# Gathering the tokens of two experts in one pass of 256-column matmuls

## The chip, the cores and the metric

The kernel runs on one core of a Trainium2 chip. The metric is the device time of one execution in microseconds (us). The kernel before takes 1973.86 us, the median of three runs (1971.27 to 1975.2). A "hi" and a "lo" below are the two fp32r parts of an fp32 number: every product of two fp32 matrices is computed as three fp32r matmuls (lo by hi, hi by lo, hi by hi).

## The reference, cut to what matters

Two decoder layers over 16 + 256 tokens of 1024 features. The first ends in a dense SwiGLU, the second in a mixture of 8 experts, of which each token takes its best two. The change touches the mixture alone:

```
probs = softmax(t @ w_router)                    # 256 tokens, 8 experts
top_p, top_i = top_k(probs, 2); top_p /= sum(top_p)
combine = sum(one_hot(top_i, 8) * top_p[..., None], axis=1)
for e in range(8):
    out += combine[:, e] * ((silu(t @ w_gate[e]) * (t @ w_up[e])) @ w_down[e])
```

with w_gate and w_up of 1024 x 3584 and w_down of 3584 x 1024 for each expert, all in fp32.

## The kernel before, in words

From about 923 us on the kernel works through the experts in turn. For each expert g it gathers the chosen tokens, at most 128 of them, into 128 slots, computes the expert for these slots, and scatters the weighted result back to the 256 tokens. (An expert with more than 128 tokens gets a further group at the end, under an If; the traced run has eight gathers, so none was taken.)

**Gather** (TensorE `gather`, L906 to L915). The selection matrix S (tokens by slots, ones and zeros; VectorE `places`, L1894, makes it with two compares) is the moving operand, 128 columns; the tokens x_hi and x_lo (2 tiles of 128 tokens each) are the stationary one. Four sources by eight blocks of 128 features are 32 matmuls at L914, which fill two banks of PSUM, X = ps[1][2:4]. ScalarE copies these to xg_hi in one instruction of 1024 columns (L1309, reached through `copy`, L1017), and VectorE subtracts to get xg_lo (L1905). For the first expert the matmuls wait for x_hi and x_lo one by one.

**An expert** is cut into seven chunks of 512 hidden columns. On TensorE a chunk (L942 to L957) is: gate, 24 matmuls of 512 columns into bank ps[0][0]; `turn`, four transposes of the hidden values of the chunk before into bank TB = ps[0][2] (L887); up, 24 matmuls into ps[0][1]; then `down` for the chunk before, 24 matmuls (L899, L901, L902) into Y = ps[1][0:2]. Chunk 0 of an expert closes the down product of the expert before it (the seam). Chunk 1 scatters the result of the expert before, into ps[0][2:4] and X. Chunk 6 begins with `slots` (L922, L924): the weight of each slot and the transpose of S go into bank MISC = ps[0][3], and ScalarE copies them out as slot_w and ST. The gather of the next expert stands in chunk 6 between up and down (L954).

**Weights** come in units of 1 MB: 6 units a chunk, 42 an expert. SyncE loads a unit into one of six raw buffers; ScalarE copies it to w_hi (L1017, from `hi_at`), VectorE subtracts to w_lo (L1566), each in one of three buffers; TensorE uses it in 12 matmuls and releases it (`units_used`). So the work of ScalarE and VectorE on a unit starts when TensorE has released the unit three places ahead of it. The instructions of each engine run in the order written; what ScalarE and VectorE do besides (ag_hi, g_sl, xg_hi on ScalarE; ag_lo, a_sl, xg_lo on VectorE) stands at fixed places between the units. In the first chunk of an expert, xg_hi comes between the first and second unit of ScalarE (L1271) and xg_lo between those of VectorE (L1851).

**Loops.** Experts 1 to 6 are one loop on each engine, with an inner loop over chunks 2 to 5; experts 0 and 7 are written out before and after it. What the loops wait on is worked out in registers from the loop's variables.

Of the kernel before, what the change touches and what calls it, by code (L numbers as in the profile page):

```python
# [50 lines left out]
START = 1  # L51

# [43 lines left out]
def trunk(nc, w, consts, where, out):  # L96

    ctx = ExitStack()
    with ctx:
# [100 lines left out]
        S = sb(moe, "S", [P, 2, P], F32R)  # L200
        ST = sb(moe, "ST", [P, 2, P], F32R)
        xg_hi = sb(moe, "xg_hi", [P, KT, P], F32R)
        xg_lo = sb(moe, "xg_lo", [P, KT, P], F32R)
# [274 lines left out]
        def norm_tmp(norm, a, b):  # L478

            if norm == 1:  # L480
                return (gT_s, aT_f)[a // 4][:, a % 4:a % 4 + b - a, width(0)]
            return sgA[:, a:b, width(norm // 2)]

# [105 lines left out]
        def _(pe):  # L589
# [283 lines left out]
            def gate_or_up(dst, at, u):  # L873
                for i in range(2):
                    u_hi, u_lo = expert_unit(at + i, u + i)
                    for k in range(4):
                        last = mm3(dst, xg_hi[:, 4 * i + k, :], xg_lo[:, 4 * i + k, :],
                                   u_hi[:, k * COLS:(k + 1) * COLS], u_lo[:, k * COLS:(k + 1) * COLS],
                                   start=(i == 0 and k == 0), stop=(i == 1 and k == 3))
                    last.then_inc(units_used, 1)  # L880
# [37 lines left out]
            def slots(g, e):  # L918

                pe.wait_ge(scatter_added, START + 2 * g + 2)  # L920
                for t in range(2):
                    nc.tensor.matmul(MISC[:, 0:1], S[:, t, :].bitcast(F32), comb[:, t, bass.ds(e, 1)], start=(t == 0), stop=(t == 1))  # L922
                for t in range(2):
                    last = nc.tensor.transpose(MISC[:, (t + 1) * P:(t + 2) * P], S[:, t, :].bitcast(F32), ident)  # L924
                last.then_inc(slots_full, 1)
# [12 lines left out]
            def expert(g, e, seam=False, more=False):  # L938

                u0, k0, at = NS + g * UPG, g * JCH, NS  # L940

                def chunk(j, first=False, final=False, scatters=False, last=False):  # L942
                    uj, k = u0 + (j * UPJ - 2), k0 + j
                    if last:
                        slots(g, e)
# [3 lines left out]
                    gate_or_up(U_, at + 6, uj + 2)  # L949
# [9 lines left out]
                pe.wait_ge(gather_hi_ready, START + g + 1)  # L959
                pe.wait_ge(gather_lo_ready, START + g + 1)  # L960
                if seam:
                    chunk(0, final=True)
                else:
                    pe.wait_ge(silu_ready, START + k0)
                    gate_or_up(G_, at, u0)
                    pe.wait_ge(hidden_ready, START + k0)
                    gate_or_up(U_, at + 2, u0 + 2)
                chunk(1, first=True, scatters=seam)
# [14 lines left out]
            gather(0, True)  # L983
# [3 lines left out]
            expert(0, 0, more=True)  # L987
            with pe.Fori(1, EXPERTS - 1) as g:
                expert(g, g, seam=True, more=True)
            expert(EXPERTS - 1, EXPERTS - 1, seam=True)  # L990
# [4 lines left out]
            for s in range(SPILLS):  # L995
                with pe.If(n_groups > s):
                    gather(EXPERTS + s, spilled=True)
                    expert(EXPERTS + s, spill[s])
# [6 lines left out]
        def _(act):  # L1005
# [253 lines left out]
            def expert(g, e, seam=False):  # L1259
# [7 lines left out]
                def chunk(j, gathers=False, scatters=False, last=False):  # L1267
                    uj, k, turns = u0 + (j * UPJ - 2), k0 + j, j - 1
                    hi_of(g, 4, turns, uj)
                    if gathers:  # L1270
                        gathered(g)  # L1271
                    hi_of(g, 5, turns, uj + 1)
                    if scatters:
                        result(g, uj)
                    if last:
                        act.wait_ge(slots_full, START + g + 1)
                        act.wait_ge(result_lo_ready, START + g + 1)
                        copy(slot_w[:, :], ps[0][:, 3, 0:1])
                        copy(ST[:, :, :], ps[0][:, 3, P:3 * P].rearrange("p (t s) -> p t s", t=2)).then_inc(slots_ready, 1)
                    for i in range(2, 4):  # L1280
                        hi_of(g, 4 + i, turns, uj + i)
                    turned(k - 1, uj)
                    silu(k, uj + 2)
                    for i in range(4, 6):
                        hi_of(g, 4 + i, turns, uj + i)

                if seam:
                    chunk(0, gathers=True)
# [17 lines left out]
            def gathered(n):  # L1306

                act.wait_ge(gather_full, START + n + 1)
                copy(xg_hi[:, :, :], ps[1][:, 2:4, :].rearrange("p b (k s) -> p (b k) s", s=P)).then_inc(gather_hi_ready, 1)  # L1309
# [13 lines left out]
            expert(0, 0)  # L1323
            with act.Fori(1, EXPERTS) as g:
                expert(g, g, seam=True)
# [3 lines left out]
            for s in range(SPILLS):  # L1329
                with act.If(n_groups > s):  # L1330
                    expert(EXPERTS + s, spill[s])
# [7 lines left out]
        def _(dve):  # L1339
# [498 lines left out]
            def expert(g, e, seam=False, more=False):  # L1838
# [8 lines left out]
                def chunk(j, start=0, gathers=False, scatters=False, last=False):  # L1847
                    uj, k = u0 + (j * UPJ - 2), k0 + j
                    for i in range(start, 4):
                        if i == 1 and gathers:  # L1850
                            gathered(g)  # L1851
                        if i == 2 and scatters:
                            result(g)
                        if i == 2 and last and more:
                            places(g + 1, g + 1, e + 1, 0)
# [10 lines left out]
                if seam:  # L1866
                    chunk(0, gathers=True)
                    chunk(1, scatters=True)
                else:
                    if type(g) is int and g == 0:  # L1870
                        gathered(0)
                        lo(3, u0 + 3)
                    else:
                        places(g, g, e, P)
                        gathered(g)
                        for i in range(4):
                            lo(i, u0 + i)
# [16 lines left out]
            def places(n, slots_read, e, first_slot):  # L1894

                dve.wait_ge(gather_full, START + n)
# [5 lines left out]
            def gathered(n):  # L1902

                dve.wait_ge(gather_hi_ready, START + n + 1)
                tt(xg_lo[:, :, :], ps[1][:, 2:4, :].rearrange("p b (k s) -> p (b k) s", s=P), xg_hi[:, :, :].bitcast(F32),  # L1905
                   ALU.subtract).then_inc(gather_lo_ready, 1)
# [19 lines left out]
            places(0, 0, 0, 0)  # L1926
# [23 lines left out]
            expert(0, 0, more=True)  # L1950
            with dve.Fori(1, EXPERTS - 1) as g:
                expert(g, g, seam=True, more=True)
            expert(EXPERTS - 1, EXPERTS - 1, seam=True)
            last_down(EXPERTS - 1)
            n_groups, spill = load_plan(dve)
            for s in range(SPILLS):
                with dve.If(n_groups > s):
                    expert(EXPERTS + s, spill[s])
# [30 lines left out]
```

## Time and profile before

| | us |
|---|---|
| median of three runs | 1973.86 |
| the profiled execution, whole | 1971.98 |
| its span, first to last instruction | 1970.0 |
| TensorE busy in the span | 1888.0 (96%) |
| VectorE busy | 1382.9 (70%) |
| ScalarE busy | 1114.6 (57%) |

The chain of work that ended last gives 52% of the span to TensorE and 1% to VectorE. A matmul's duration in the trace holds its way through the array, and the next one starts long before it ends; what a matmul costs in a sequence is the distance from its start to the next one's start. Rows with a count (x16) merge neighbours of one kind. Each row has start, duration, engine, line, operation, out<-in and count; what stands in brackets is idle time and what ended it.

### The profile page before, as it was taken

How to read it: one execution, taken by the hardware profiler on the slowest of the kernel's cores; microseconds unless marked ns; L12 is line 12 of the kernel's file. 1: busy time of each engine (PE TensorE's matmuls, PEld its weight loads, DVE VectorE, ACT ScalarE, POOL GpSimd, SP SyncE). 2: the span in 40 equal slices, each digit the busy share in tenths (PEclk: the TensorE clock that was granted, in tenths of full speed). 3: DMA queues.
4: the chain of work that ended last, by engine and by line, in shares of the span. 5: the costliest groups of instructions: out<-in, count | busy, mean ns of one | idle time of the engine just before them, and what ended most of it. 6: DMA issues, size and time to landing. Idle time of an engine off the chain costs nothing.

```text
span 1970.0 us, 28868 instructions
## 1 busy us (share of the span) xinstructions
PE 1888.0 (96%) x11195; PEld 1664.4 (84%) x11195; DVE 1382.9 (70%) x1134; ACT 1114.6 (57%) x850; POOL 6.3 (0%) x15
## 2 busy tenths in 40 slices
PE   7999999899989899998999999999999999999995
PEld 6889999899988899997888888888888888888883
DVE  2555556644554556566788888888888888888885
ACT  3634344533454453444777667776767677676773
POOL 0000000000000000000000000000000000000000
PEclk9889999999998999997999999999999999999998
DMA  9636633454566548343899999999999999999991
GB/s 218 182 107 184 160 124 134 150 171 147 183 110 155 145 124 204 125 169 124 297 365 333 354 359 327 367 340 347 357 332 360 334 351 361 337 348 349 337 366 73
DMA packets 218448, 488.19 MB, mean 248 GB/s; under 512 B 7884, under 2 KB 12744, under 8 KB 218360
## 3 DMA queue, kind: packets, MB, share of 16 engines
q1 hardware_dynamic: 216464, 482.44, 73.3%
q10 hardware_dynamic: 1400, 2.33, 0.5%
q0 software_dynamic: 496, 2.17, 0.3%
q8 instruction: 66, 1.08, 0.2%
q14 instruction: 22, 0.18, 0.0%
HBM read 483.66 MB, written 1.05 MB: 246 GB/s over the span
## 4 chain that ended last, share of the span: by engine, by line
PE 52%; DVE 1%; issue 0%; ACT 0%; DVEq 0%; ACTq 0%
PE ps L595 11%; PE ps L597 11%; PE ps L596 11%; PE ps L899 5%; PE ps L902 5%; PE ps L901 5%; PE ps L914 1%; PE ps L887 1%; PE ps L934 0%; PE ps L839 0%; PE ps L935 0%; DVE w_lo L1566 0%; PE ps L848 0%; PE ps L922 0%; DVE h_tok L1545 0%
## 5 line engine op out<-in xcount | busy, mean ns | idle before, releaser
L1566 DVE TENSOR_TENSOR w_lo<-raw,w_hi 128x2048 fp32r<-128x2048 f32 x336 | 763.3, 2289 | 153.9 <-ACT w_hi L1017 152.4
L1017 ACT ACTIVATE w_hi<-raw 128x2048 fp32r<-128x2048 f32 x336 | 639.1, 1918 | 197.9 <-PE ps L902 103.8
L595 PE MATMUL ps<-hT_hi,w_lo 128*128 128x272 f32 (+1 forms) x1392 | 407.7, 293 | 27.4 <-DVE hT_lo L1518 13.6
L361 DVE TENSOR_TENSOR w_lo<-raw,w_hi 128x2048 fp32r<-128x2048 f32 (+2 forms) x131 | 279.4, 2143 | 217.1 <-ACT w_hi L354 211.7
L596 PE MATMUL ps<-hT_lo,w_hi 128*128 128x272 f32 (+1 forms) x1392 | 406.0, 292 | 0.0
L597 PE MATMUL ps<-hT_hi,w_hi 128*128 128x272 f32 (+1 forms) x1392 | 405.4, 291 | 0.0
L595 PE MATMUL ps<-w_hi,xg_lo 128*128 128x512 f32 x896 | 361.0, 403 | 3.2 <-DVE xg_lo L1905 3.2
L597 PE MATMUL ps<-w_hi,xg_hi 128*128 128x512 f32 x896 | 355.1, 396 | 0.0
L596 PE MATMUL ps<-w_lo,xg_hi 128*128 128x512 f32 x896 | 354.9, 396 | 0.0
L354 ACT ACTIVATE w_hi<-raw 128x2048 fp32r<-128x2048 f32 (+2 forms) x131 | 233.9, 1793 | 183.0 <-PE ps L597 140.7
L595 PEld LDWEIGHTS ps<-hT_hi,w_lo 128*128 128x128 f32 x1392 | 269.2, 193 | 32.3 <-issue 22.6
L596 PEld LDWEIGHTS ps<-hT_lo,w_hi 128*128 128x128 f32 x1392 | 268.9, 193 | 0.1
L597 PEld LDWEIGHTS ps<-hT_hi,w_hi 128*128 128x128 f32 x1392 | 268.2, 193 | 0.0
L595 PEld LDWEIGHTS ps<-w_hi,xg_lo 128*128 128x128 f32 x896 | 169.2, 189 | 41.0 <-issue 3.6
L597 PEld LDWEIGHTS ps<-w_hi,xg_hi 128*128 128x128 f32 x896 | 169.1, 189 | 40.8
L596 PEld LDWEIGHTS ps<-w_lo,xg_hi 128*128 128x128 f32 x896 | 169.4, 189 | 37.4
L899 PE MATMUL ps<-w_hi,ag_lo 128*128 128x512 f32 x448 | 177.6, 396 | 1.8 <-DVE ag_lo L1835 1.8
L901 PE MATMUL ps<-w_lo,ag_hi 128*128 128x512 f32 x448 | 177.1, 395 | 0.0
L902 PE MATMUL ps<-w_hi,ag_hi 128*128 128x512 f32 x448 | 177.1, 395 | 0.0
L899 PEld LDWEIGHTS ps<-w_hi,ag_lo 128*128 128x128 f32 x448 | 84.2, 188 | 25.9 <-DVE ag_lo L1835 2.0
L902 PEld LDWEIGHTS ps<-w_hi,ag_hi 128*128 128x128 f32 x448 | 84.2, 188 | 20.1
L901 PEld LDWEIGHTS ps<-w_lo,ag_hi 128*128 128x128 f32 x448 | 84.3, 188 | 18.0
(260 smaller groups left out, 1867.3 us busy)
## 6 DMA issues: line engine op xcount, KB each, us to landing
raw<-in_moe_w_gate SPq DMA_DIRECT2D x112, 1024.0 KB, 7.1
raw<-in_moe_w_up SPq DMA_DIRECT2D x112, 1024.0 KB, 7.3
raw<-in_moe_w_down SPq DMA_DIRECT2D x112, 1024.0 KB, 6.2
raw<-in_w_in SPq DMA_DIRECT2D x63, 1024.0 KB, 8.6
raw<-in_ffn_w_gate SPq DMA_DIRECT2D x10, 1024.0 KB, 5.1
raw<-in_ffn_w_up SPq DMA_DIRECT2D x10, 1024.0 KB, 5.1
raw<-in_ffn_w_down SPq DMA_DIRECT2D x10, 1024.0 KB, 5.1
raw<-in_w_pa SPq DMA_DIRECT2D x8, 1024.0 KB, 5.1
```

Of the source, the lines that this page charges most:

```text
L354: nc.scalar.activation(w_hi[:, u % HALVES, 0:k * n], raw[:, u % RAW, 0:k * n], ACT.Copy).then_inc(hi_ready, 1)
L361: nc.vector.tensor_tensor(w_lo[:, u % HALVES, 0:k * n], raw[:, u % RAW, 0:k * n], w_hi[:, u % HALVES, 0:k * n].bitcast(F32), ALU.subtract) ...
L595: nc.tensor.matmul(dst, l_lo, r_hi, start=start, stop=False)
L596: nc.tensor.matmul(dst, l_hi, r_lo, start=False, stop=False)
L597: return nc.tensor.matmul(dst, l_hi, r_hi, start=False, stop=stop)
L887: last = nc.tensor.transpose(TB[:, i * P:(i + 1) * P], a_sl[:, i * P:(i + 1) * P], ident)
L899: last = nc.tensor.matmul(Y[:, q, :], ag_lo[:, 2 * i + kk, :], u_hi[:, o:o + COLS], start=first and i == 0 and kk == 0, stop=False)
L901: nc.tensor.matmul(Y[:, q, :], ag_hi[:, 2 * i + kk, :], u_lo[:, o:o + COLS], start=False, stop=False)
L902: last = nc.tensor.matmul(Y[:, q, :], ag_hi[:, 2 * i + kk, :], u_hi[:, o:o + COLS], start=False, stop=final and i == 1 and kk == 1)
L914: last = nc.tensor.matmul(X[:, k // 4, (k % 4) * P:(k % 4 + 1) * P], x_[:, t, k * P:(k + 1) * P], S[:, t, :], start=(i == 0 and k % 4 == 0 ...
L1017: return nc.scalar.activation(dst, src, ACT.Copy, **kw)
L1566: tt(w_lo[:, at % HALVES, :], raw[:, at % RAW, :], w_hi[:, at % HALVES, :].bitcast(F32), ALU.subtract).then_inc(lo_ready, 1)
```

## The change

The gather is done for two experts at once. S gets a further axis (one selection per expert, 256 columns in all), so do xg_hi and xg_lo. A pair's gather is done in two halves of 16 matmuls with 256 moving columns, one for each half of the features: the first fills ps[1][2:4], as before, the second ps[0][2:4], which are the banks TB and MISC. Each copy out takes one half of the features of one expert (512 columns, in four pieces of 128), so there are four copies on ScalarE and four subtractions on VectorE for a pair where there were two of 1024 columns each. In the first chunk of a pair the first expert's copies stand between the first and second unit, the second expert's between the second and third. ScalarE's copy for the second expert waits until VectorE has read the same banks for the first. The matmuls and copies of the experts are otherwise as before, and so are the weights' loads.

Added waits on TensorE: before a pair's gather, that the hidden values were copied out of TB and the slots out of MISC; before the first `turn` after it, that all four subtractions are done. The loop runs over pairs (1 and 2), its body has two experts; pairs 0 and 3 are written out.

```diff
-        S = sb(moe, "S", [P, 2, P], F32R)
+        S = sb(moe, "S", [P, 2, 2, P], F32R)
...
-            def gather(n, first_gather=False, spilled=False):
+            def gather(m, n, first_gather=False, spilled=False):
-                pe.wait_ge(places_ready, START + n + 1)
+                pe.wait_ge(places_ready, START + m + 1)
                 pe.wait_ge(scatter_added, START + 2 * n + (2 if spilled else 0))
-                for i, (x_, t) in enumerate(((x_hi, 0), (x_hi, 1), (x_lo, 0), (x_lo, 1))):
-                    if first_gather:
-                        pe.wait_ge((x_hi_ready, x_lo_ready)[i // 2], t + 1)
-                    for k in range(KT):
-                        last = nc.tensor.matmul(X[:, k // 4, (k % 4) * P:(k % 4 + 1) * P], x_[:, t, k * P:(k + 1) * P], S[:, t, :],
-                                                start=(i == 0 and k % 4 == 0), stop=(i == 3 and k % 4 == 3))
-                last.then_inc(gather_full, 1)
+                for half in range(2):
+                    for i, (x_, t) in enumerate(((x_hi, 0), (x_hi, 1), (x_lo, 0), (x_lo, 1))):
+                        if first_gather and half == 0:
+                            pe.wait_ge((x_hi_ready, x_lo_ready)[i // 2], t + 1)
+                        for k in range(4):
+                            f = (4 * half + k) * P
+                            last = nc.tensor.matmul(ps[1 - half][:, 2 + k // 2, (k % 2) * 2 * P:(k % 2 + 1) * 2 * P], x_[:, t, f:f + P],
+                                                    S[:, t, :, :].rearrange("p e s -> p (e s)"),
+                                                    start=(i == 0 and k % 2 == 0), stop=(i == 3 and k % 2 == 1))
+                    last.then_inc(gather_full, 1)
...
                     pe.wait_ge(silu_ready, START + k)
-                    gate_or_up(G_, at + 4, uj)
+                    gate_or_up(G_, at + 4, uj, o)
+                    if moved:
+                        pe.wait_ge(gather_lo_ready, START + 4 * m + 4)
                     turn(k - 1)
...
                     if last and more:
-                        gather(g + 1)
+                        pe.wait_ge(hidden_lo_ready, START + k)
+                        pe.wait_ge(slots_ready, START + g + 1)
+                        gather(m + 1, g + 1)
...
-            with pe.Fori(1, EXPERTS - 1) as g:
-                expert(g, g, seam=True, more=True)
+            with pe.Fori(1, PAIRS - 1) as m:
+                expert(m, m * 2, m * 2, 0, seam=True)
+                expert(m, m * 2 + 1, m * 2 + 1, 1, seam=True, more=True)
...
@@ ScalarE, an expert's chunk
                     hi_of(g, 4, turns, uj)
                     if gathers:
-                        gathered(g)
+                        gathered(m, 0)
                     hi_of(g, 5, turns, uj + 1)
+                    if gathers:
+                        gathered(m, 1)
...
@@ ScalarE, expert 0 (not at a seam)
-                    gathered(g)
-                    for i in range(HALVES if type(g) is int and g == 0 else 0, 4):
+                    gathered(m, 0)
+                    for i in range(HALVES if m == 0 else 0, 4):
                         hi_of(g, i, 0, u0 + i)
+                    gathered(m, 1)
                     silu(k0, u0 + 2)
...
+            def gathered(m, o):
+                for half in range(2):
+                    act.wait_ge(gather_full, START + 2 * m + half + 1)
+                    if o:
+                        act.wait_ge(gather_lo_ready, START + 4 * m + half + 1)
+                    copy(xg_hi[:, o, 4 * half:4 * half + 4, :], gathered_in(half, o)).then_inc(gather_hi_ready, 1)
...
@@ VectorE: places makes both experts' selections
-                for t in range(2):
-                    ins = ts_(S[:, t, :], iota[:, first_slot:first_slot + P], rank[:, t, bass.ds(e, 1)], None, ALU.is_equal)
+                for t in range(2):
+                    for o, e in enumerate(experts):
+                        ins = ts_(S[:, t, o, :], iota[:, first_slot:first_slot + P], rank[:, t, bass.ds(e, 1)], None, ALU.is_equal)
...
+                    tt(xg_lo[these], gathered_in(half, o), xg_hi[these].bitcast(F32), ALU.subtract).then_inc(gather_lo_ready, 1)
```

## Rows read from the trace of the kernel before

**Rows 1.** Busy time by engine in a stretch of expert work: count, clock, DMA share, GB/s.
```profile
core 0: us, PE busy (x) PEld busy (x) DVE busy (x) ACT busy (x) POOL busy (x), PEclk, DMA share, GB/s
1160.00:1800.00 640.00, 640.00 (x2921) 520.43 (x2920) 546.69 (x315) 449.72 (x305) 0.00 (x0) 1.00 0.96 348
```

**Rows 2.** Waits of TensorE, 950 to 1970 us: total, times, longest.
```profile
PE ps L934 <- DVE y_lo L1911: 2.5, 1, 2.5
PE ps L899 <- DVE ag_lo L1835: 1.8, 1, 1.8
```

**Rows 3.** Timeline of TensorE around the gather for expert 2.
```profile
1171.18 0.40 PE L597 MATMUL ps<-w_hi,xg_hi 128*128 128x512 f32 x1
1171.41 1.90 PE L914 MATMUL ps<-S,x_hi 128*128 128x128 f32 x16
1173.15 1.95 PE L914 MATMUL ps<-S,x_lo 128*128 128x128 f32 x16
1174.93 0.45 PE L899 MATMUL ps<-w_hi,ag_lo 128*128 128x512 f32 x1
```

**Rows 4.** Timeline of TensorE: fp32r matmuls of 256 columns, the first and the last of 37.
```profile
897.73 0.28 PE L597 MATMUL ps<-zT_hi,w_hi 128*128 128x256 f32 x1
...
901.99 0.28 PE L597 MATMUL ps<-zT_hi,w_hi 128*128 128x256 f32 x1
```

**Rows 5.** Timeline of TensorE: matmuls of 256 columns whose operands are plain fp32.
```profile
690.45 1.03 PE L743 MATMUL ps<-v_tok,eT 128*128 128x256 f32 x4
691.32 1.03 PE L747 MATMUL ps<-srT,qT 128*128 128x256 f32 x4
```

**Rows 6.** Busy time and clock in the stretch of the first gather; columns as in rows 1.
```profile
926.00:933.00 7.00, 4.26 (x20) 4.08 (x20) 6.18 (x20) 1.65 (x3) 0.00 (x0) 0.50 0.00 0
```

**Rows 7.** Timeline from the first gather to expert 0.
```profile
922.51 0.48 DVE L1899 TENSOR_SCALAR S<-tab,rank 128x128 fp32r<-128x128 f32 x2 [0.79 <-DVE plan_f L1813]
...
923.21 3.64 PE L914 MATMUL ps<-S,x_hi 128*128 128x128 f32 x16
...
926.65 3.62 PE L914 MATMUL ps<-S,x_lo 128*128 128x128 f32 x16
...
929.70 2.29 DVE L1566 TENSOR_TENSOR w_lo<-raw,w_hi 128x2048 fp32r<-128x2048 f32 x1
...
931.91 1.22 DVE L1905 TENSOR_TENSOR xg_lo<-ps,xg_hi 128x1024 fp32r<-128x1024 f32 x1
...
933.49 0.77 PE L595 MATMUL ps<-w_hi,xg_lo 128*128 128x512 f32 x1 [3.23 <-DVE xg_lo L1905]
```

**Rows 8.** Timeline of expert 0's first units, to the start of its chunk 1.
```profile
938.08 1.92 ACT L1017 ACTIVATE w_hi<-raw 128x2048 fp32r<-128x2048 f32 x1 [6.76 <-PE ps L597]
...
943.74 4.50 DVE L1566 TENSOR_TENSOR w_lo<-raw,w_hi 128x2048 fp32r<-128x2048 f32 x2 [1.42 <-ACT w_hi L1017]
...
946.22 0.43 PE L595 MATMUL ps<-w_hi,xg_lo 128*128 128x512 f32 x1
```

**Rows 9.** Groups of instructions, 950 to 1960 us: copies of 512 columns (busy, mean ns).
```profile
L1835 DVE TENSOR_TENSOR ag_lo<-ps,ag_hi 128x512 fp32r<-128x512 f32 x56 | 38.3, 684 | 0.0
...
L1017 ACT ACTIVATE ag_hi<-ps 128x512 fp32r<-128x512 f32 x56 | 33.5, 599 | 72.7 <-PE ps L887 72.7
```

**Rows 10.** Timeline after that gather: third unit of chunk 0, and up.
```profile
1182.82 2.29 DVE L1566 TENSOR_TENSOR w_lo<-raw,w_hi 128x2048 fp32r<-128x2048 f32 x1 [0.52 <-ACT w_hi L1017]
...
1186.54 0.48 PE L595 MATMUL ps<-w_hi,xg_lo 128*128 128x512 f32 x1
```

**Rows 11.** Timeline of an ordinary chunk: the first unit of down.
```profile
1151.08 4.49 DVE L1566 TENSOR_TENSOR w_lo<-raw,w_hi 128x2048 fp32r<-128x2048 f32 x2 [1.32 <-ACT w_hi L1017]
...
1153.33 0.40 PE L597 MATMUL ps<-w_hi,xg_hi 128*128 128x512 f32 x1
...
1153.56 0.39 PE L899 MATMUL ps<-w_hi,ag_lo 128*128 128x512 f32 x1
```

**Rows 12.** Register instructions of ScalarE's wait for a unit (L1022).
```profile
L1022 ACTq ALU_OP  x191: 35/35/53, 958.1 to 1926.5; - x191
```

**Rows 13.** The busiest chunk for the DMA queues; columns as in rows 1.
```profile
1243.00:1260.00 17.00, 17.00 (x77) 13.69 (x76) 14.77 (x8) 12.15 (x9) 0.00 (x0) 1.00 1.01 365
```

More of the change, by code:

```diff
@@ L936, in scatter, with expert, chunk @@
                     last.then_inc(scatter_full, 1)
-            def expert(g, e, seam=False, more=False):
+            def expert(m, g, e, o, seam=False, more=False):
                 u0, k0, at = NS + g * UPG, g * JCH, NS
-                def chunk(j, first=False, final=False, scatters=False, last=False):
+                def chunk(j, first=False, final=False, scatters=False, last=False, moved=False):
                     uj, k = u0 + (j * UPJ - 2), k0 + j
                     if last:
-                        slots(g, e)
+                        slots(g, e, o)
                     pe.wait_ge(silu_ready, START + k)
-                    gate_or_up(G_, at + 4, uj)
+                    gate_or_up(G_, at + 4, uj, o)
+                    if moved:
+                        pe.wait_ge(gather_lo_ready, START + 4 * m + 4)
                     turn(k - 1)
-                    gate_or_up(U_, at + 6, uj + 2)
+                    gate_or_up(U_, at + 6, uj + 2, o)
                     if scatters:
@@ L982, in _ @@
             pe.wait_ge(dve_done, NSETS - 1)
-            gather(0, True)
+            gather(0, 0, True)
             pe.wait_ge(act_done, NSETS)
@@ L986, in _ @@
             pe.wait_ge(comb_ready, 1)
-            expert(0, 0, more=True)
-            with pe.Fori(1, EXPERTS - 1) as g:
-                expert(g, g, seam=True, more=True)
-            expert(EXPERTS - 1, EXPERTS - 1, seam=True)
+            expert(0, 0, 0, 0)
+            expert(0, 1, 1, 1, seam=True, more=True)
+            with pe.Fori(1, PAIRS - 1) as m:
+                expert(m, m * 2, m * 2, 0, seam=True)
+                expert(m, m * 2 + 1, m * 2 + 1, 1, seam=True, more=True)
+            expert(PAIRS - 1, EXPERTS - 2, EXPERTS - 2, 0, seam=True)
+            expert(PAIRS - 1, EXPERTS - 1, EXPERTS - 1, 1, seam=True)
             last_down(EXPERTS - 1)
@@ L996, in _ @@
                 with pe.If(n_groups > s):
-                    gather(EXPERTS + s, spilled=True)
-                    expert(EXPERTS + s, spill[s])
+                    gather(PAIRS + s, EXPERTS + s, spilled=True)
+                    expert(PAIRS + s, EXPERTS + s, spill[s], 0)
                     last_down(EXPERTS + s)
@@ L1257, in turned, with expert @@
                 copy(ag_hi[:, :, :], TB4).then_inc(hidden_hi_ready, 1)
-            def expert(g, e, seam=False):
+            def expert(m, g, e, o, seam=False):
                 u0, k0 = NS + g * UPG, g * JCH
@@ L1322, in _ @@
             act.sem_inc(result_hi_ready, START + 1)
-            expert(0, 0)
-            with act.Fori(1, EXPERTS) as g:
-                expert(g, g, seam=True)
+            expert(0, 0, 0, 0)
+            expert(0, 1, 1, 1, seam=True)
+            with act.Fori(1, PAIRS) as m:
+                for o in range(2):
+                    expert(m, m * 2 + o, m * 2 + o, o, seam=True)
             last_down(EXPERTS - 1)
@@ L1836, in turned, with expert @@
                    ALU.subtract).then_inc(hidden_lo_ready, 1)
-            def expert(g, e, seam=False, more=False):
+            def expert(m, g, e, o, seam=False, more=False):
                 u0, k0 = NS + g * UPG, g * JCH
@@ L1849, in chunk @@
                     for i in range(start, 4):
-                        if i == 1 and gathers:
-                            gathered(g)
+                        if i in (1, 2) and gathers:
+                            gathered(m, i - 1)
                         if i == 2 and scatters:
@@ L1866, in expert @@
                 if seam:
-                    chunk(0, gathers=True)
+                    chunk(0, gathers=(o == 0))
                     chunk(1, scatters=True)
                 else:
[L1870 to L1877, printed above, removed]
+                    if m:
+                        places(m, g, (e,), P)
+                    gathered(m, 0)
+                    for i in range(0 if m else 3, 4):
+                        lo(i, u0 + i)
+                    gathered(m, 1)
                     for i in range(4, 6):
@@ L1892, in last_down, with places, gathered @@
                     add(g + 1, t)
-            def places(n, slots_read, e, first_slot):
-                dve.wait_ge(gather_full, START + n)
+            def places(m, slots_read, experts, first_slot):
+                dve.wait_ge(gather_full, START + 2 * m)
                 dve.wait_ge(slots_full, START + slots_read)
                 for t in range(2):
-                    ins = ts_(S[:, t, :], iota[:, first_slot:first_slot + P], rank[:, t, bass.ds(e, 1)], None, ALU.is_equal)
+                    for o, e in enumerate(experts):
+                        ins = ts_(S[:, t, o, :], iota[:, first_slot:first_slot + P], rank[:, t, bass.ds(e, 1)], None, ALU.is_equal)
                 ins.then_inc(places_ready, 1)
[L1902 to L1906, printed above, removed]
+            def gathered(m, o):
+                for half in range(2):
+                    dve.wait_ge(gather_hi_ready, START + 4 * m + 2 * o + half + 1)
+                    these = (slice(None), o, slice(4 * half, 4 * half + 4))
+                    tt(xg_lo[these], gathered_in(half, o), xg_hi[these].bitcast(F32), ALU.subtract).then_inc(gather_lo_ready, 1)
             def result(n):
@@ L1925, in _ @@
             dve.sem_inc(scatter_added, START + 2)
-            places(0, 0, 0, 0)
+            places(0, 0, (0, 1), 0)
             r = number[1, "x_tok"]
@@ L1949, in _ @@
             lo(HALVES - 1, NS + HALVES - 1)
[L1950 to L1953, printed above, removed]
+            expert(0, 0, 0, 0)
+            expert(0, 1, 1, 1, seam=True, more=True)
+            with dve.Fori(1, PAIRS - 1) as m:
+                expert(m, m * 2, m * 2, 0, seam=True)
+                expert(m, m * 2 + 1, m * 2 + 1, 1, seam=True, more=True)
+            expert(PAIRS - 1, EXPERTS - 2, EXPERTS - 2, 0, seam=True)
+            expert(PAIRS - 1, EXPERTS - 1, EXPERTS - 1, 1, seam=True)
             last_down(EXPERTS - 1)
```

40 lines of the change are left out of this document (20 added, 20 removed).

## The prediction

> **What bounds the kernel now.** I read the windows first, since a change in the expert part can pay only if the engine it relieves never rests there. From 1160 to 1800 us TensorE is busy 640 of 640 us at the full clock; VectorE is at 85% (546.69 / 640), ScalarE at 70% [rows 1]. Then its waits: in the last 1020 us there are two, 4.3 us together, both behind the last expert [rows 2]. So the start-to-start distances of TensorE's matmuls are the time, and each microsecond taken out of its sequence shortens the run, as long as units and copies still come in time. The timeline of one gather gives what the change works on.
>
> **Gathers at the full clock.** One expert's 32 matmuls of 128 columns take 1174.93 - 1171.41 = 3.52 us, 110 ns from start to start [rows 3]. fp32r matmuls of 256 columns, with a new stationary operand each time as in the gather, stand (901.99 - 897.73) / 36 = 118 ns apart [rows 4]. A pair's gather has 32 of them: 3.79 us. Seven of the eight gathers run at the full clock; three pair gathers take their place:
>
> 7 x 3.52 - 3 x 3.79 = 24.64 - 11.37 = **13.3 us less**.
>
> The bound on the other side is plain fp32, whose 256 columns stand (691.32 - 690.45) / 4 = 217 ns apart [rows 5]. I take 118 ns because S, x_hi and x_lo are declared fp32r like the operands of rows 4, while those of rows 5 are not.
>
> Here a rule speaks against the change. The measured 110 ns at 128 columns and 118 at 256 say that width is nearly free [rows 3, 4]. The Trainium skill ("TensorE: Matmul & The Clock Gate", section "Back-to-back issue gap") gives N / 2.4 + 2.5 ns for an isolated matmul at the fast clock, 56 ns at 128 columns and 109 at 256: by that, two narrow matmuls cost the same as one wide, and the gathers would give nothing. The trace disagrees at 128 columns by a factor of two. The same page's "LDWEIGHTS" section puts a load of 128 columns at 128 / 1.2 = 107 ns, with which 110 ns agrees; by the two together the sum stays as it is.
>
> **The first gather.** It runs at a granted clock of 0.50 [rows 6], 3.44 us for 16 matmuls [rows 7], 215 ns each. Before it `places` now makes four selections: two took 0.48 us, so two more put the start 0.4 us later. At this clock 256 columns cost between 215 ns, as now, and 2 x 118 = 236, so 6.9 to 7.6 us for the same 32 matmuls, some 0.5 us more with the wait for the second x_lo, which now falls at the twelfth matmul and not the twenty-fourth. The gather thus ends between 930.6 and 931.6 in place of about 930.1. What the first expert waits for is not this: VectorE is busy with a unit from 929.70 to 931.99, and only then subtracts [rows 7]. Of its two subtractions the second needs ScalarE's copy, ready by 932.2 at the latest. Two of 684 ns [rows 9] take 1.37 us in place of 1.22: **0.15 us more**.
>
> **Expert 0.** ScalarE's copies for expert 1 are put behind its unit that ends at 940.00, ahead of the silu and of the next unit; that one's w_lo ends at 943.74 + 2.29 = 946.03, and chunk 1 starts at 946.22 [rows 8]. Nothing covers a delay: TensorE already starts at the moment the unit is ready. Two copies of 599 ns [rows 9], overlapping a little, cost 1.0 to 1.2 us; I take **1.1 us more**. The least is 0 (if ScalarE got there earlier), the most 1.4 (if VectorE's two subtractions, 1.37 us, were late too; they fit in the time before its next unit).
>
> **The seams between pairs** (three). I carry the timeline on. The first expert's copies: one behind the first half of the gather, one behind the second, before ScalarE's next unit. Then that unit (to about 1180.1), and the second expert's two copies to 1181.3; VectorE has its unit until 1182.5 and the two subtractions until 1183.9. The third unit's w_lo, which started at 1182.82, starts then, 1.1 us later, and ends at 1186.2. TensorE wants it at 1186.54, and 0.24 us later with the longer gather [rows 10]: a margin of 0.6 us. The fourth unit has more. The added wait before `turn` is met at 1183.9, TensorE arrives at 1186.4. The two added waits before the gather are for copies made microseconds earlier, and queue nothing. VectorE's `places` makes two more selections in chunk 6 (0.48 us [rows 7]), two units ahead of need. **0 us**; from below it can't be a gain, since TensorE rests nowhere; from above, if the strided reads took twice the time, the 4 x 0.68 us more on VectorE would cost 2.7 - 0.6 = 2.1 us a seam.
>
> **The seams inside pairs** (four) lose their gather, which stood between up and down and covered the first down unit. In an ordinary chunk that unit's w_lo ends at 1151.08 + 2.29 = 1153.37, and down starts at 1153.56, 0.23 us after the matmul before it, the normal distance: no stall, but no slack [rows 11]. Chunk 6 of these experts becomes such a chunk. **0 us**, at most about 0.1 each.
>
> **DMA.** 336 units of 1 MB, 352 million bytes, now have to come in some 12 us less. The busiest chunk took 365 GB/s without a wait [rows 13], the mean is 348 [rows 1] and would be 352. **0 us**.
>
> **The sum.** -13.3 + 0.15 + 1.1 = **-12.05 us**. The profiled execution took 1971.98 us (span 1970.0), so 1959.9 like for like; it lies 1.9 us below the median of 1973.86. From the median: **1961.8 us**.
>
> **The rivals.**
> *Pair seams stall.* The copies come late, by strided reads or a wait that I placed wrongly, 1 to 2 us in each of three seams: 1965 to 1968. For it: VectorE at 85%, four copies where one stood, three buffers. Against: the 0.6 us above.
> *Columns are paid in full.* The 256-column gather runs like rows 5, 217 ns. Then 24.64 - 3 x 6.94 = 3.8 us are saved; the first gather takes 13.9 us in place of 6.9 at half clock, which nothing hides: expert 0 starts at about 939.1 in place of 933.5, 5.6 us; with the 1.1 us that is 2.9 us more: 1976.8. For it: the operand's doubled axis. Against: its type, and rows 4.
> *The DMA queues are the bound.* The bytes are the same, so the time stays at 1974. For it: a share of 0.96 to 1.01 [rows 1, 13]. Against: no wait for a landing in ScalarE's list, and 365 GB/s reached.
> *The chunks get longer: slower.* Place: turn, ag_hi, silu, w_hi, w_lo, down, in every chunk at its edge [rows 11]. The loops now count pairs, and an expert's number is 2m or 2m + 1; each register instruction so added costs ScalarE 35 ns [rows 12] if it falls on that chain. The loop has 28 chunks. It eats the gain at 12.05 / 28 = 0.43 us a chunk, twelve instructions, and is slower beyond; at sixteen, 0.56 us a chunk: 15.7 - 12.05 = 3.6 us more, 1977.5. Against: register instructions run ahead while the engine works.
> *The clock comes back in the first gather.* Now the 32 narrow matmuls pass at 0.50 without a rise. Expert 0's first 48 matmuls take 946.22 - 933.49 = 12.7 us [rows 7, 8], where 48 at the 0.23 us of the full clock [rows 3] would take 11.0; the rest is the slow clock's. If the wider gather raises the clock and it holds over the pause, up to 1.7 us more are gained: 1960.1.
>
> **How the numbers follow.** Forecast 0.70, clock 0.06, pair seams 0.12: faster 0.88. Columns 0.04, DMA queues 0.04: same 0.08 (within 0.2%, 3.9 us, about what a measurement of this kernel tells from no change). Longer chunks 0.04: slower 0.04. The range: below, the clock's 1.7 us, no cost at expert 0 and the scatter of the runs, 1957.5; above, the pair seams, 1968.5.
>
> **What would show it.** 128 matmuls at the gather's line with 256 columns, 118 ns apart, three groups of 3.8 us; a wait of TensorE of about 1.1 us at expert 0's chunk 1 for w_lo, and otherwise no wait from 950 us to the last expert; the first matmul of expert 0 within 0.3 us of 933.5. Wrong, if the 256-column distance is over 130 ns, or TensorE's list of waits shows a row of several microseconds at the seams, or distances of over 240 ns at each first down matmul.

## The result and the profile after

The changed kernel takes 1959.02 us, the median of five runs (1952.18 to 1960.22), against 1971.91 for the kernel before in the same comparison: 12.9 us less, a ratio of 0.9924 (95% interval 0.9909 to 0.9938). Its profiled execution took 1959.02 us, with a span of 1957.3. TensorE is busy 1874.0 us in it (14.0 less), VectorE 1382.0 and ScalarE 1114.8 (both within 1 us of before).

The windows of the same stretch as [rows 1], after the change: TensorE still rests nowhere, VectorE has gone from 546.69 to 552.76 us, since more chunks now fall into the stretch.

```profile
1160.00:1800.00 640.00, 640.00 (x2884) 517.61 (x2883) 552.76 (x322) 455.21 (x315) 0.00 (x0) 1.00 0.97 351
```

TensorE's waits from 915 us on (in total, times, longest). The first row below is expert 0's start, there before as well (3.23 us [rows 7]); the second stands behind the last expert, as in [rows 2]; the third is new. The rows left out are y_lo's 2.5 us, as in [rows 2], and two of 0.5 us and less ahead of expert 0.

```profile
PE ps L600 <- DVE xg_lo L1929: 4.4, 1, 4.4
...
PE ps L904 <- DVE ag_lo L1858: 1.8, 1, 1.8
PE ps L600 <- DVE w_lo L1589: 0.8, 1, 0.8
...
```

The timeline of TensorE around the gather for experts 6 and 7, which answers to [rows 3]: four groups of eight matmuls, the first, the third, and the down matmul behind them.

```profile
1666.97 1.12 PE L921 MATMUL ps<-S,x_hi 128*128 128x256 f32 x8
...
1668.88 1.12 PE L921 MATMUL ps<-S,x_hi 128*128 128x256 f32 x8
...
1670.80 0.40 PE L904 MATMUL ps<-w_hi,ag_lo 128*128 128x512 f32 x1
```

A pair's gather takes 1670.80 - 1666.97 = 3.83 us, 120 ns a matmul, where two gathers took 7.04.

To take the whole apart I cut each trace at the same instructions. All numbers are us; the stage of the experts runs from the first matmul of expert 0 to the first of the last `down`.

| | before | after | difference |
|---|---|---|---|
| start of the router's matmuls | 910.38 | 908.08 | -2.3 |
| from there to expert 0 | 23.10 | 23.17 | +0.1 |
| the experts | 1006.14 | 993.87 | -12.3 |
| to the end of the last addition | 12.16 | 12.55 | +0.4 |
| pause of VectorE before the layer norm | 5.00 | 8.06 | +3.1 |
| layer norm, output | 13.22 | 11.57 | -1.7 |

The experts' stage was forecast at -13.3 + 1.1 = -12.2. By expert, each counted from its own first `up` matmul to the next one's: each odd one went from 126.7 to 127.0 (its gather is 3.8 and not 3.5 us), each even one but the first from 126.7 to 123.15, and expert 0, counted from its very first matmul, from 126.36 to 123.80.

The last row is not work. In all 13 traces of this document the last transfer of the output is issued 8.4 us after VectorE's first layer norm instruction; it then takes 4.4 us to land before and 2.7 us after. It took 4.4 to 4.7 us in three traces (before, again_before, before_pairs) and 2.7 in the other ten, two of which are of the old form too; why, I did not find.

### The profile page after: what moved, and what is told of

Its sections match the earlier page's. It is cut to its first block, busy times and chain, and to the rows that moved or that the text cites. A ratio compares the mean times of both kernels' runs of the same rounds, so it can differ in the third digit from the quotient of the medians.

```text
span 1957.3 us, 28505 instructions
## 1 busy us (share of the span) xinstructions
PE 1874.0 (96%) x11067; PEld 1647.2 (84%) x11067; DVE 1382.0 (71%) x1142; ACT 1114.8 (57%) x858; POOL 6.3 (0%) x15
## 4 chain that ended last, share of the span: by engine, by line
PE 51%; DVE 1%; issue 1%; ACT 1%; DVEq 0%; ACTq 0%
PE ps L600 11%; PE ps L602 11%; PE ps L601 11%; PE ps L904 5%; PE ps L907 5%; PE ps L906 5%; PE ps L892 1%; PE ps L921 1%; DVE w_lo L1589 0%; PE ps L942 0%; PE ps L943 0%; PE ps L844 0%; PE ps L853 0%; ACT w_hi L1032 0%; PE ps L930 0%
```

## The experiments

Each ran with a profile and, unless said, is compared by its median. The runs of before beside them had medians of 1972.29 (both kernels once more, `narrow`, `early`), 1972.36 (`before_pairs`, `before_roomy`, `before_skip`, `twice`) and 1970.33 (`skip`, `lo_later`, `all_three`). "The changed kernel" below is its 1959.05, 13.2 under before in the first of these comparisons; for the last three runs I also give the distance to it with each taken against its own before.

**Both kernels once more.** No edit.

> The kernel before, unchanged, for the scatter from one execution to the next. Theory (the 2.3 us that the changed kernel gained ahead of 335 us and the 3.1 us that it lost between the last scatter and the last layer norm are not the gather's): if they are chance, this trace differs from the first one of before by 1 to 3 us at the same places, around 50 us and in VectorE's 5.0 us pause before the layer norm. Rival: both belong to the changed kernel, and this trace repeats 5.0 us and the first matmul of the router at 910.4 us within 0.3 us.

> The changed kernel, unchanged. From the first matmul of expert 0 to the first of the last down unit it takes 996.8 us again (within 0.3), since TensorE rests nowhere in it but for 0.93 us at expert 0's chunk 1. Theory of chance: VectorE's pause before the layer norm and the router's first matmul (908.1 us) move by 1 to 3 us. Rival: the pause stays at 8.1 us in this kernel and at 5.0 in the one before, being the price of a longer program.

Before: 1972.7 us (ratio 1.0, interval 0.999 to 1.001). After: 1959.05 (0.993, 0.9914 to 0.9947). What lies between router and end repeats: the experts take 1006.19 and 993.65 (the 996.8 of the expectation counts 12 matmuls further, to the last unit; counted so the two traces have 996.8 and 996.6), the way to expert 0 is 23.11 and 23.17, the pause 4.87 and 7.35. The start of the router does not: 910.91 and 904.46. So the theory of chance holds for the router; of the 3.1 us in the pause it can claim only the 0.7 by which it moved. Over all 13 traces the router's start goes with the time that TensorE's clock spent at 0.50 before it, whichever kernel runs: 910.1 to 910.9 with 61.4 us of it, 908.0 to 908.2 with 58.0, 907.4 to 907.6 with 54.6, 905.0 with 51.2, 903.5 to 904.5 with 47.8. The router moves by half the slow time, as a doubled rate would have it, and most of the scatter between executions of one kernel goes the same way: of the executions of before on record, the thirty with a mean clock of 0.973 took 1973.0 us on average, the five with 0.977 took 1966.6.

**narrow: the width alone undone.**

```diff
-                            last = nc.tensor.matmul(ps[1 - half][:, 2 + k // 2, (k % 2) * 2 * P:(k % 2 + 1) * 2 * P], x_[:, t, f:f + P],
-                                                    S[:, t, :, :].rearrange("p e s -> p (e s)"),
...
+                            for e in range(2):
+                                c = ((k % 2) * 2 + e) * P
+                                last = nc.tensor.matmul(ps[1 - half][:, 2 + k // 2, c:c + P], x_[:, t, f:f + P], S[:, t, e, :],
...
```

> Only the width is undone: a pair's gather in 64 matmuls of 128 columns in place of 32 of 256; banks, copies, waits and loops stay those of the change. Theory (the width is the gain, 110 ns for each matmul of up to 128 columns and 118 for 256): each of the three gathers at the full clock takes 64 x 0.110 = 7.04 us in place of 3.8, 9.8 us more, and the first one, at half clock with 0.215 us each, ends some 5 to 7 us later; together 14 to 17 us more than the changed kernel, 1973 to 1976, as slow as the kernel before or 1 to 2 us slower. Rival (the new banks and the half copies bring part of it, for instance by an earlier first copy): clearly under 1971.

1974.13 us, a ratio of 1.0002 to the kernel before (0.9988 to 1.0016): 15.1 us more than the changed kernel. A gather in its timeline, first matmul and the down matmul behind it:

```profile
1679.52 1.90 PE L923 MATMUL ps<-S,x_hi 128*128 128x128 f32 x16
...
1686.61 0.45 PE L904 MATMUL ps<-w_hi,ag_lo 128*128 128x512 f32 x1
```

7.09 us for 64 matmuls, 111 ns each; the odd experts take 130.3 in place of 127.0, and expert 0 starts 28.83 us after the router, 5.66 later. 3 x 3.28 + 5.66 = 15.5, and expert 0's stage is 0.5 longer. So the width is the whole gain; the new banks and half copies bring nothing.

**early: expert 1's copies of the first pair ahead of the unit.**

```diff
                     gathered(m, 0)
+                    if m == 0:
+                        gathered(m, 1)
                     for i in range(HALVES if m == 0 else 0, 4):
                         hi_of(g, i, 0, u0 + i)
-                    gathered(m, 1)
+                    if m:
+                        gathered(m, 1)
```

(and the same on VectorE)

> In the first pair alone, the copies and subtractions for expert 1 are moved from behind the fourth unit to directly behind those for expert 0, where ScalarE and VectorE rest for some 6 us until TensorE releases a unit. Theory: the wait of 0.93 us at expert 0's chunk 1 goes, since nothing then stands before the silu; 0.9 to 1.0 us less from expert 0 to the end, and expert 0 starts as before. Rival (that wait is a late weight unit, as before the change, and not the copies): it stays within 0.2 us.

1958.19 us, 0.9 less than the changed kernel's 1959.05 beside it, which the times alone would not settle. The trace does: the wait for w_lo is gone from TensorE's list (its longest row is shown), chunk 1 starts 234 ns after the matmul before it where it was 1165, and expert 0's stage is 122.73 in place of 123.69 and 123.80.

```profile
PE ps L600 <- ACT xg_hi L1032: 4.5, 1, 4.5
...
```

**before_pairs: the kernel before, its loops written by pairs.**

```diff
-            with pe.Fori(1, EXPERTS - 1) as g:
-                expert(g, g, seam=True, more=True)
+            expert(1, 1, seam=True, more=True)
+            with pe.Fori(1, EXPERTS // 2 - 1) as m:
+                for o in range(2):
+                    expert(m * 2 + o, m * 2 + o, seam=True, more=True)
+            expert(EXPERTS - 2, EXPERTS - 2, seam=True, more=True)
```

(TensorE; the loops of ScalarE and VectorE likewise)

> The kernel before, gathers and copies unchanged, with only its loops over experts written as in the changed kernel: pairs 1 and 2 in a loop whose body has two experts (numbers 2m and 2m + 1), the others written out. Theory (what the changed kernel gained ahead of the router, some 2 us at its first wait for weights at about 50 us, and lost in VectorE's pause before the layer norm, 2.4 to 3.1 us, comes with the longer program): the router starts 1 to 3 us earlier than 910.4, the pause is 7 to 8 us, and the experts take 1006.1 us as before. Rival 1 (they come with the gather or the tiles): 910.4, 5.0, and the same time as before. Rival 2 (more register work in each wait lengthens the chunks): experts take longer than 1006.1 us, by 28 times what a chunk pays.

1969.67 us (ratio 0.9992, 0.9982 to 1.0002). The experts take 1006.26 us, so rival 2 falls: numbers of 2m + 1 cost the chunks nothing. The pause is 4.86, so it isn't the loops that lengthened it. Its router starts at 903.70, with 47.8 us of slow clock. But one thing at the start does go with this form: TensorE's wait near 50 us, in the first layer, for the tile sgA from ScalarE. In the traces before, before_pairs and after, one row each:

```profile
50.86 3.99 PE L790 MATMUL ps<-sgA,a 16*128 16x272 f32 x8 [4.00 <-ACT sgA L1017]
```
```profile
48.95 3.48 PE L790 MATMUL ps<-sgA,a 16*128 16x272 f32 x8 [2.01 <-ACT sgA L1020]
```
```profile
49.38 2.99 PE L795 MATMUL ps<-sgA,a 16*128 16x272 f32 x8 [2.01 <-ACT sgA L1032]
```

This matmul starts at 50.9 to 51.3 in the four traces whose experts are looped singly, at 48.6 to 49.4 in all nine that are written by pairs. In those the weights of these first microseconds land earlier: the tenth unit at 40.6 in place of 46.0 (after, before). The distance holds: the matmul behind TensorE's next pause of 1.9 us, near 96 us, starts at 98.4 to 98.8 in the four and at 95.9 to 96.3 in the nine, and the clock's stretch at 0.50 near 50 us lasts 10.2 us in the four and 6.8 in the nine. Since before_pairs differs from before in nothing but its loops, this is their work.

**before_roomy: two unused tiles in the kernel before.**

```diff
+        S_more = sb(moe, "S_more", [P, 2, P], F32R)
...
+        xg_more = sb(moe, "xg_more", [P, 2, KT, P], F32R)
```

> The kernel before, with two further tiles that nothing uses, of the sizes that the change adds to the selection and the gathered tokens. Theory (the program's length, not the tiles' places, moves the first 50 us): router at 910.4 to 910.9 and 1972, as before. Rival (the place of the tiles): router 1 to 3 us earlier, the time 2 us lower.

1972.05 us (0.9999, 0.9987 to 1.0012), the wait near 50 us as in the kernel before (50.94). The tiles' places are not it. Its router at 907.35 goes with 54.6 us of slow clock. Its pause before the layer norm, though, is 6.06 us, and from router to end it takes 1.4 us more than before; so in the kernel before that pause is not a fixed 5.0 us.

**before_skip and skip: one branch around the three overfull groups**, in the kernel before and in the changed one.

```diff
+            with dve.If(n_groups > 0):
                 for s in range(SPILLS):
                     with dve.If(n_groups > s):
                         ...
                     dve.end_ifs()
+            dve.end_ifs()
```

(on each of the four engines; the inner lines are only moved in)

> The kernel before, with one further branch on each engine around the three groups for overfull experts: where there is none, all three are passed in one jump in place of three. In the first trace VectorE's three branches of before were 0.6 and 2.5 us apart and the last one 0.2 us ahead of the next instruction, in a pause of 5.0 us. Theory (each far jump waits for instructions to be fetched, 0.6 to 3 us): the pause falls to 2.5 to 4.5 us. Rival (the pause is the reading of the plan, which stays): 4.8 to 5.0.

> The changed kernel, with one branch on each engine around the three groups for overfull experts. Theory (far jumps cost VectorE its pause of 7.4 to 8.1 us, of which 2.3 are the reading of the plan): the pause falls to 3 to 5 us, 3 to 4 us less in all. Rival: the fetch behind a single jump takes as long; the pause stays over 7.

before_skip: 1970.26 us (0.9993, 0.998 to 1.0006), pause 4.56, just over the 2.5 to 4.5 that the theory said and hardly under the 4.87 to 5.00 of before. skip: 1953.78 us (0.992, 0.9894 to 0.9946), pause 4.56 in place of 7.35 and 8.06. VectorE's first layer norm instruction in before, in after and in skip:

```profile
1956.79 0.70 DVE L1388 BATCH_NORM_STATS2 stats<-h_tok 128x6 f32<-128x512 f32 x1 [5.00 <-issue]
```
```profile
1945.73 0.69 DVE L1411 BATCH_NORM_STATS2 stats<-h_tok 128x6 f32<-128x512 f32 x1 [8.06 <-issue]
```
```profile
1937.59 2.47 DVE L1417 BATCH_NORM_STATS2 stats<-h_tok 128x6 f32<-128x512 f32 x4 [4.56 <-issue]
```

From router to end the skip trace has 1045.6 us, after and again_after 1049.2 and 1048.3: 3.1 us less, as expected. Its median is 5.3 under the changed kernel's, but before was faster beside it as well: with each taken against its own before it is 3.3.

The trace shows the branches too, as instructions of VectorE's queue; the rows give how many there are and when the first and the last one start, in before and in after:

```profile
L1957 DVEq COMPARE_BRANCH  x3: 56/56/56, 1953.4 to 1956.5; - x3
```
```profile
L1983 DVEq COMPARE_BRANCH  x3: 56/56/68, 1939.3 to 1942.6; - x3
```

The first branch comes 1.6 us after the last addition in all 13 traces; that is the reading of the plan. From there the three branches take, each to the next instruction, 0.6, 2.5 and 0.3 us in before and 0.6, 2.7 and 3.2 us in after. In the other traces the second takes 2.4 to 3.6 us in either form; the third takes 0.3 us in every trace of the old form and 2.5 to 3.0 in every one of the changed. Behind a single branch it is 3.0 to 3.1 us. So what the change lengthened is, for the most part, the third jump.

**twice: 0.5 us more on ScalarE in each chunk.**

```diff
+                copy(spare[:, :].rearrange("p (k s) -> p k s", s=P), TB4)
                 copy(ag_hi[:, :, :], TB4).then_inc(hidden_hi_ready, 1)
```

> The changed kernel with one more copy of 512 columns on ScalarE (0.6 us, some 0.5 from start to start) ahead of ag_hi in each of the 56 chunks. Theory (turn, ag_hi, silu, w_hi, w_lo, down is at its edge in an ordinary chunk, and only the gathers cover it): each chunk but the three that have a gather between up and down, and those at either end, waits about 0.5 us at its first down matmul; some 52 x 0.5 = 26 us more, 1985. Rival (there is slack that the trace doesn't show): under 5 us more.

1981.21 us, 22.2 more than the changed kernel; the experts take 1017.66 against 993.8, 23.9 more. At 45 first down matmuls TensorE now comes 0.60 us after the matmul before, 0.37 more than 233 ns, and 16.6 us in all; its list has them as a row of 45. So the edge is there, a little softer than I said (0.37 of 0.5). Of the other 7.3 us, 5.2 are waits of 0.1 to 0.2 us just behind, at the second matmul of `down` (38 times) and at the first of the next gate (7 times), and 1.8 are expert 0's, where the clock stood at 0.50 for 6.8 us in place of 3.4.

```profile
PE ps L905 <- DVE w_lo L1591: 9.2, 45, 0.3
```

**lo_later: the weight unit behind the first subtraction**, VectorE.

```diff
                     gathered(m, 0)
-                    for i in range(0 if m else 3, 4):
+                    for i in range(0 if m else 2, 4):
...
-            lo(HALVES - 1, NS + HALVES - 1)
             expert(0, 0, 0, 0)
```

> The changed kernel; VectorE's unit that stood ahead of the first subtraction for expert 0 (2.29 us, 927.40 in its trace) now comes behind it. Theory: TensorE waits for this subtraction alone, whose second half could start when ScalarE's copy ends at 927.45; expert 0 starts at 928.9 in place of 931.25, 2.3 us earlier relative to the router, 2.0 to 2.4 us less in all; the unit itself is needed only 6 us later. Rival (the gather or another wait, for the combine weights, ends as late): less than 1 us.

1956.39 us (0.9926, 0.9902 to 0.9949), 2.7 less than the changed kernel, or 0.7 with each taken against its own before: the times do not settle it. From router to end its trace has 1046.7 us against 1049.2 and 1048.3. The start came only 1.23 us earlier (21.94 behind the router): in this execution the clock rose 2.4 us before expert 0, too late to quicken the gather, whose last matmul started at 930.01. In exchange it did not fall again in the pause of 1.7 us, and expert 0's stage is 122.36, 1.4 less. So the 1.6 to 2.5 us of the trace are near the 2.0 to 2.4 that I expected, but by luck: 1.4 of them are the clock's, of which the theory knew nothing.

**all_three: early, lo_later and skip together.**

> The changed kernel with all three: copies of the first pair early, the unit behind the subtraction, one branch around the overfull groups. Theory: the three pieces lie in different stretches and add up: 1.0 + 2.2 + 3.5 = 6.7 us less than the changed kernel, about 1952. Rival: the earlier start is given back, since with both edits in VectorE's order the unit for expert 0's third 12 matmuls is late: some 2 us of it lost.

1950.14 us (ratio to before 0.9903, 0.9874 to 0.9932), 8.9 less than the changed kernel (7.0 with each taken against its own before), the fastest of all. Its subtractions follow the copy at once, and expert 0 starts 20.94 us behind the router:

```profile
927.51 2.69 DVE L1941 TENSOR_TENSOR xg_lo<-ps,xg_hi 128x512 fp32r<-128x512 f32 x4
...
929.14 0.47 PE L602 MATMUL ps<-w_hi,xg_lo 128*128 128x512 f32 x1 [2.25 <-ACT xg_hi L1036]
```

From router to end it has 1040.7 us against 1048.3 and 1049.2, so 7.6 to 8.5 less. The third unit was not late. What it has beyond the 6.7 that I expected is the clock: in the shorter pause (2.25 us) it stays at 1.00, and expert 0's stage is 121.40 where early has 122.73.

## Why the prediction came out as it did

**The gathers** (-13.3). Right: four even experts about -3.5 each (expert 0 without its new wait), three odd ones +0.3, together -13.4. The distance is 120 ns where [rows 4] gave 118. `narrow` shows that the width is the cause. The rule that spoke against the change, the Trainium skill's N / 2.4 + 2.5 ns for an isolated matmul ("TensorE: Matmul & The Clock Gate", section "Back-to-back issue gap"), does not hold for this stream: it gives 56 ns at 128 columns, and in `narrow` they stand 111 ns apart.

**Expert 0's chunk 1** (+1.1). Right in kind and nearly in size: 1165 ns before its first matmul in place of 235, 0.93 us, and `early` takes it away. ScalarE's order is as forecast: the copies between the unit and the silu, the next unit late.

```profile
937.68 1.07 ACT L1032 ACTIVATE xg_hi<-ps 128x512 fp32r<-128x512 f32 x2
...
940.56 5.62 ACT L1032 ACTIVATE w_hi<-raw 128x2048 fp32r<-128x2048 f32 x3
```
```profile
944.93 0.48 PE L600 MATMUL ps<-w_hi,xg_lo 128*128 128x512 f32 x1 [0.77 <-DVE w_lo L1589]
```

**The first gather** (+0.15). The sum is right, 23.17 against 23.10 us, the way to it is not. `places` and the unit of VectorE are as forecast, and this unit, not the gather, sets the start of expert 0. The gather ended at about 926.8, 5.5 us behind its start and not 7 to 8, since the clock rose in it; its error did not show because nothing waited for its end. (That expert 0 starts at 931.25, and not within 0.3 us of 933.5 as I said, is the router's earlier start.) The timeline, and the windows of the pause and of expert 0's first matmuls:

```profile
920.20 0.87 DVE L1921 TENSOR_SCALAR S<-tab,rank 128x128 fp32r<-128x128 f32 x4 [0.79 <-DVE plan_f L1836]
...
925.69 1.12 PE L921 MATMUL ps<-S,x_lo 128*128 128x256 f32 x8
...
927.40 2.29 DVE L1589 TENSOR_TENSOR w_lo<-raw,w_hi 128x2048 fp32r<-128x2048 f32 x1
...
929.61 1.28 DVE L1929 TENSOR_TENSOR xg_lo<-ps,xg_hi 128x512 fp32r<-128x512 f32 x2
...
931.25 0.77 PE L600 MATMUL ps<-w_hi,xg_lo 128*128 128x512 f32 x1 [4.44 <-DVE xg_lo L1929]
```
```profile
924.50:931.00 6.50, 2.31 (x20) 2.11 (x18) 5.86 (x20) 1.19 (x2) 0.00 (x0) 1.00 0.05 4
931.30:934.40 3.10, 3.10 (x8) 2.42 (x9) 0.00 (x0) 0.00 (x0) 0.00 (x0) 0.50 0.84 322
```

The rival of the clock was thus half true: it came back (1.00 from 924.3 on) and fell again as expert 0 began, after a pause of 4.4 us, so that the first matmuls still ran at 0.50. The gain that I gave that rival appears only where the pause is shorter, in lo_later and all_three.

**The seams between pairs** (0). Right, with a margin of 0.9 us where I had 0.6: the third unit's w_lo ends at 1679.16 + 2.29 = 1681.45, up starts at 1682.36.

```profile
1679.16 4.49 DVE L1589 TENSOR_TENSOR w_lo<-raw,w_hi 128x2048 fp32r<-128x2048 f32 x2
```
```profile
1682.36 0.48 PE L600 MATMUL ps<-w_hi,xg_lo 128*128 128x512 f32 x1
```

**The seams inside pairs, the edge of each chunk** (0). Right: the first down matmul of their chunk 6 comes 234 to 240 ns after the one before. That it is an edge is shown by `twice`; that the change did not push it, by `before_pairs`.

**DMA** (0). Right: 351 GB/s, and no wait.

**The step that failed is the sum itself, -13.3 + 0.15 + 1.1 = -12.05: it has no term for anything ahead of the router or behind the last expert, and gives no reason for putting both at nothing.** "The chunks get longer" asked what a longer program does to the chunks, and there it did nothing; what it did was at two other places, of 1 to 3 us each.

First, the end. VectorE's pause before the layer norm is 4.9 to 6.1 us in the four old traces with three branches and 7.0 to 8.1 in all six traces of the changed form without the outer branch. The difference is spent in the jumps over code that never runs, whose bodies the change altered, and nearly all of it in the third (0.3 us in place of 2.5 to 3.2); one outer branch takes the pause to 4.6. Why the third jump was short before and is long now is not shown. Pause and what follows it together are 17.6 to 18.4 us in those four traces and 18.6 to 19.6 in the six, so the end of the kernel has lost about 1.0 us net; the landing of the output, 2.7 us in these six and 4.4 to 4.7 in three of the four, hides the rest.

Secondly, the front. From router to end the changed kernel has 10.4 to 11.5 us less, its medians 12.9 and 13.2 less; the other 2 us lie before the router, where nothing of the gather runs. They come with the pairwise code. before_pairs, which changes nothing else, has the earlier start near 50 and 96 us, and its median is 2.7 under before with the same time from router to end; narrow's is 1.8 over it with 4.1 more from router to end. The size is less sure: the interval of before_pairs reaches 1.0002, and its router at 903.7 owes much to less slow clock. Among executions with the same mean clock before_pairs averages 1.4 to 1.5 us less (1971.6 against 1973.0 at 0.973, 1969.3 against 1970.8 at 0.974, 1965.2 against 1966.6 at 0.977). In the table's 2.3 us, 1.7 are the clock's shorter stretch at 0.50 near 50 us. Why the first weights land earlier I did not find.

So the forecast time of 1961.8 was 2.8 us too high: 1.9 us of that is the base, whose median fell from 1973.86 to 1971.91 with two further runs, and 0.9 us the gain, 12.9 for 12.05. That the gain came out so near is in part luck: the mechanism that was forecast brings 12.2 us in the traces, and beside it the front gives 2.3 and the end takes 1.8, which nearly cancel.

## What to carry to other kernels

Where the start-to-start distance hardly depends on the columns (111 ns at 128, 120 at 256 here), pair up work that shares its stationary operand; the gain is the number of matmuls saved times that distance, less the little that each wider one takes more, and can be read from two rows. Then look at what the wider step now makes come at once (four copies in one gap), and give them the place where the engine rests. And ask of a longer program what it does where code is jumped over, at the end and at the start, not only in the loop.

## What the runs showed of the hardware

- An fp32r matmul with a stationary operand of its own took 110 to 111 ns from start to start at 128 columns, 118 to 120 at 256 and 233 at 512, at the full clock. At half clock, 128 columns took 215 [rows 7].
- TensorE's clock stayed at 0.50 through 32 matmuls of 128 columns, 6.9 us without a rest, and through 64 in narrow; it rose within the 32 of 256 columns in all seven traces that have these. It fell again after a pause of 4.4 us (after), and not after those of 1.7 (lo_later) and 2.25 (all_three).
- Three jumps over unexecuted code took VectorE 3.3 to 4.5 us in the old form and 5.4 to 6.5 in the changed; each of them 0.3 to 3.6 us. A single jump over the same three bodies took 3.0 to 3.1.
- With the experts' loops written by pairs, the tenth 1 MB unit of weights landed at 39.1 to 41.0 us, and at 44.7 to 46.0 with them looped singly.
- With the same program, the start of the router varied by 3.6 us between two executions, with the time at half clock before it (58.0 and 47.8 us).
- The last transfer of the output took 2.7 us from issue to landing in ten traces and 4.4 to 4.7 in three.
